# Two retention phases hand their PSUM banks over one by one, and a gated projection moves from the gate's chunks to a stretch of its own

## The reference, cut to what matters

```python
# first block, layer by layer (layer 0 for x and ctx, 512 rows; layer 1 for x, 256 rows)
hx = _rmsnorm(x, norm_w) * (1 + scale[:, None]) + shift[:, None]
a_h, a_b, a_c, a_z, q, k, v, r_z = _split_in(hx @ w_in)
q_h = _axial_rope(_heads(q), row_pos, col_pos)
k_h = _axial_rope(_heads(k), row_pos, col_pos) * k_scale
o = _bidir_retention(q_h, k_h, _heads(v), lg_f, lg_b, s_f, s_b)
y_ret = _ret_out(o, r_z, ret_norm_w)
x = x + gate[:, None] * (jnp.concatenate([y_conv, y_ret], axis=-1) @ w_out)
# end of the second block
x = x + rms_norm(f, ln_ffn_post[i])          # f = (silu(g) * u) @ w_down
gate = jax.nn.sigmoid(rms_norm(x, ln_pli[i]) @ w_pli_gate[i])
x = x + gate * (p[i] @ w_pli_proj[i])        # p is 256 x 256, w_pli_proj 256 x 2048
```

## Time and profile before

| what | us |
|---|---|
| median of 3 runs | 3027.54 (3026.38 to 3034.44) |
| the profiled execution, its own time | 3030.63 |
| its span, first to last instruction | 3028.8 |
| PE busy, share of the span | 2950.3, 97% |
| DVE busy | 1828.4, 60% |
| ACT busy | 1367.8, 45% |

### The profile page before, as it was taken

One profiled execution on the slowest core, in us unless ns is written; L12 is line 12 of the kernel. 1 busy time (PEld: TensorE's weight loads), 2 busy tenths in 40 slices (PEclk: granted clock), 3 DMA queues, 4 the chain that ended last, 5 costly groups with the idle time before them and its releaser, 6 DMA issues.

```text
span 3028.8 us, 41594 instructions
## 1 busy us (share of the span) xinstructions
PE 2950.3 (97%) x14729; PEld 2477.7 (82%) x14729; DVE 1828.4 (60%) x2315; ACT 1367.8 (45%) x1890; POOL 111.3 (4%) x114
## 2 busy tenths in 40 slices
PE   7999999999999999999999999999999999999999
PEld 4678887788887889988888899997788888878877
DVE  6878878788774345544445677665545445444454
ACT  6732222433343244434444577674544444434353
POOL 0000000000110000001110000000000000000000
PEclk9999999999999999999999999999999999999999
DMA  8855545444554225543334555555555555555545
GB/s 279 305 186 188 184 173 191 153 161 151 199 183 163 93 100 187 186 134 109 106 108 145 168 156 155 158 160 171 158 186 182 185 182 183 185 195 188 188 154 167
DMA packets 144277, 515.12 MB, mean 170 GB/s; under 512 B 16240, under 2 KB 16288, under 8 KB 142256
## 3 DMA queue, kind: packets, MB, share of 16 engines
q1 hardware_dynamic: 141264, 495.01, 49.2%
q0 software_dynamic: 2912, 18.74, 1.7%
HBM read 511.55 MB, written 2.13 MB: 170 GB/s over the span
## 4 chain that ended last, share of the span: by engine, by line
PE 57%; ACT 2%; DVE 2%; issue 2%; DMA 0%; ACTq 0%; DVEq 0%; SPq 0%
PE main L1582 47%; PE main L1575 6%; PE aux L1535 1%; ACT w_hi L580 1%; PE aux L1717 0%; PE aux L1708 0%; DVE w_lo L983 0%; PE aux L1555 0%; DVE h_lo L1105 0%; DMA raw<-in_w_sb 0%; ACT L804 0%; PE aux L1768 0%; ACT h_hi L690 0%; PE main L1655 0%; DVE u L1267 0%
## 5 line engine op out<-in xcount | busy, mean ns | idle before, releaser
L983 DVE TENSOR_TENSOR w_lo<-raw,w_hi 128x1024 fp32r<-128x1024 f32 x836 | 1039.1, 1246 | 876.2 <-ACT w_hi L580 865.7
L580 ACT ACTIVATE w_hi<-raw 128x1024 fp32r<-128x1024 f32 x836 | 880.1, 1058 | 1297.0 <-PE main L1582 973.8
L1582 PE MATMUL main<-w_hi,h_hi 128*128 128x512 f32 (+1 forms) x1472 | 561.9, 382 | 6.4 <-DVE h_lo L1232 3.1
L1582 PE MATMUL main<-w_lo,h_hi 128*128 128x512 f32 (+1 forms) x1472 | 552.4, 375 | 0.0
L1582 PE MATMUL main<-w_hi,h_lo 128*128 128x512 f32 (+1 forms) x1472 | 552.4, 375 | 0.0
L1582 PE MATMUL main<-w_hi,act_hi 128*128 128x512 f32 (+1 forms) x1408 | 536.4, 381 | 10.6 <-ACT u L720 6.5
L1582 PE MATMUL main<-w_hi,act_lo 128*128 128x512 f32 (+1 forms) x1408 | 528.2, 375 | 0.0
L1582 PE MATMUL main<-w_lo,act_hi 128*128 128x512 f32 (+1 forms) x1408 | 527.7, 375 | 0.0
L1575 PE MATMUL main<-act_hi,w_hi 128*128 128x256 f32 (+1 forms) x960 | 321.7, 335 | 3.7 <-DVE act_lo L1087 2.8
L1575 PE MATMUL main<-act_hi,w_lo 128*128 128x256 f32 (+1 forms) x960 | 320.5, 334 | 0.0
L1575 PE MATMUL main<-act_lo,w_hi 128*128 128x256 f32 (+1 forms) x960 | 320.4, 334 | 0.0
(11 more groups left out here) (269 smaller groups left out, 2491.2 us busy)
## 6 DMA issues: line engine op xcount, KB each, us to landing
raw<-in_w_ffn_up SPq DMA_DIRECT2D x176, 512.0 KB, 3.3
gates<-in_w_side SPq DMA_DIRECT2D x128, 512.0 KB, 3.4
raw<-in_w_in_ret SPq DMA_DIRECT2D x128, 512.0 KB, 4.0
raw<-in_w_in_conv SPq DMA_DIRECT2D x120, 512.0 KB, 4.1
raw<-in_w_out SPq DMA_DIRECT2D x96, 512.0 KB, 3.3
raw<-in_w_ffn_down SPq DMA_DIRECT2D x88, 512.0 KB, 4.2
raw<-in_w_mod SPq DMA_DIRECT2D x64, 512.0 KB, 4.7
raw<-in_w_sb SPq DMA_DIRECT2D x64, 384.0 KB, 3.1
```

Source lines behind the costliest of these rows:

```text
L580: A(w_hi[:, slot, :], raw[:, slot, :], ACT.Copy).then_inc(hi_split, 1)
L983: V.tensor_tensor(out=w_lo[:, slot, :], in0=raw[:, slot, :], in1=w_hi[:, slot, :].bitcast(F32), op=ALU.subtract).then_inc(lo_split, 1)
L1582: ins = mm(bank[:, c0:c1], x, w_part[:, slot, j * n + c0:j * n + c1], start=(k == 0 and j == 0 and i == 0), stop=(k == (7 if name == "gate ...
```

## The change

**Bank by bank.** In the last piece of every chunk of `in0_ret` and `in1_ret`, PE now signals `bank_done` after each of the banks 0, 1 and 2, as it did in `out0` only. ACT waits for the signal of bank 0 and of bank 2, DVE for that of bank 1; DVE's copy of bank 3 still waits for the whole chunk. The counts of `out0` are offset (`banks`).

**The projection.** The four pieces of `w_pli_proj` leave the gate's chunks and become a phase `proj` of 4 pieces between `ffn_down` and `gate`, whose chunks now have 8 pieces. PE runs two of them straight after `ffn_down`, one between the transposes of groups 0 and 1, and one behind those; the identity matmuls there are gone. ACT copies each product from `main` to a new SBUF tile `pp` (`proj_out`), and DVE multiplies by `pp` at the end. The fetch and the split of p move into the last chunk of `ffn_down`. Four splits of weight pieces on ACT and DVE now stand between the steps of the norm, where one stood behind the first two groups.

```diff
@@ -34,7 +34,8 @@
     ("in1_ret", 8, 8, 1024), ("out1", 4, 8, 1024), ("sb", 8, 8, 768), ("dil", 8, 8, 768),
-    ("out2", 4, 8, 1024), ("ffn_up", 22, 8, 1024), ("ffn_down", 4, 22, 1024), ("gate", 4, 9, 1024),
+    ("out2", 4, 8, 1024), ("ffn_up", 22, 8, 1024), ("ffn_down", 4, 22, 1024),
+    ("proj", 1, 4, 1024), ("gate", 4, 8, 1024),
 ]
@@ -267,6 +268,7 @@
         p_lo = sb(pli, "p_lo", [P, 2 * 256], F32R)
+        pp = sb(pli, "pp", [P, 2, D])
         pli.close()
@@ -321,13 +323,15 @@
             done_a[name], done_d[name] = na, nd
-            evacuated = {"mod0": 0, "in0_conv": 8}.get(name, c)
+            evacuated = {"mod0": 0, "in0_conv": 8, "proj": 0}.get(name, c)
             nd += evacuated
...
         paired = {n: n not in ("in0_conv", "in0_ret", "in1_ret", "out0") for n, *_ in PHASES}
+        banks = {"in0_ret": 0, "out0": 24, "in1_ret": 36}
@@ -557,7 +561,7 @@
             pool.dma_start(frow[:], a["rows"][2, :].partition_broadcast(P)).then_inc(s["fr_in"], 16)
-            pool.wait_ge(s["eaten"], chunk_end("ffn_down", 3))
+            pool.wait_ge(s["eaten"], chunk_end("ffn_down", 2) + 13)
             pool.dma_start(ptok[:], a["pT"]).then_inc(s["pt_in"], 16)
@@ -678,10 +682,10 @@
-            def prepare(n, A_cols, k):
+            def prepare(n, A_cols, k, groups=None):
                 j = prep_index(n) - 3
-                for kg in norm_groups(k):
+                for kg in norm_groups(k) if groups is None else groups:
                     m = 4 * prep_index(n) + kg
@@ -713,9 +717,9 @@
                 if k == 0:
-                    act.wait_ge(eaten, chunk_end(f"in{L}_ret", e))
                     act.wait_ge(s["rt_y"], 8 * L + e + 1)
                     for t in range(0, 4, 2):
+                        act.wait_ge(s["bank_done"], banks[f"in{L}_ret"] + 3 * e + t + 1)
                         lo, n = (128, 256) if t >= T else (0, 512)
@@ -955,18 +959,36 @@
             phase("ffn_up", lambda k: prepare(5, ln("ffnpre"), k), ffn_up)
-            phase("ffn_down", lambda k: ffn_up(21, 1, k), lambda e, par, k: plain_out("ffn_down", e, par, k))
+            def down_step(e, par, k):
+                plain_out("ffn_down", e, par, k)
+                if isinstance(e, int) and e == 2 and k == 17:
+                    act.wait_ge(s["pt_in"], 16)
+                    A(p_hi[:], ptok[:], ACT.Copy).then_inc(s["px_h"], 1)
+            def proj_out(k):
+                act.wait_ge(eaten, BASE["proj"] + k + 1)
+                for t in range(2):
+                    ins = A(pp[:, t, k * 512:(k + 1) * 512], main[2 * (k % 2) + t][:, :], ACT.Copy)
+                ins.then_inc(s["pj_done"], 1)
+            phase("ffn_down", lambda k: ffn_up(21, 1, k), down_step)
             sqrt_table()
...
             norm_root(6, 2)
-
-            def gate_start(k):
-                prepare(7, ln("pli"), k)
-                if k == 5:
-                    act.wait_ge(s["pt_in"], 16)
-                    A(p_hi[:], ptok[:], ACT.Copy).then_inc(s["px_h"], 1)
-
-            phase("gate", gate_start, gate, last=True)
+            first = BASE["proj"] + LEAD
+            split(first, first % SLOTS)
+            proj_out(0)
+            prepare(7, ln("pli"), 0, (0,))
+            split(first + 1, (first + 1) % SLOTS)
+            proj_out(1)
+            prepare(7, ln("pli"), 0, (1,))
+            split(first + 2, (first + 2) % SLOTS)
+            proj_out(2)
+            split(first + 3, (first + 3) % SLOTS)
+            proj_out(3)
+            phase("gate", lambda k: prepare(7, ln("pli"), k, () if k == 0 else None), gate, last=True)
             gate(3, 1, 0)
@@ -1119,7 +1141,19 @@
-                if k == 0:
+                if k == 0 and n == 7:
+                    first = BASE["proj"] + LEAD
+                    x_group(0)
+                    split(first, first % SLOTS)
+                    x_group(1)
+                    low(0)
+                    split(first + 1, (first + 1) % SLOTS)
+                    x_group(2)
+                    low(1)
+                    split(first + 2, (first + 2) % SLOTS)
+                    x_group(3)
+                    split(first + 3, (first + 3) % SLOTS)
+                elif k == 0:
                     x_group(0)
@@ -1171,8 +1205,11 @@
                 if k == 0:
-                    dve.wait_ge(eaten, chunk_end(f"in{L}_ret", e))
                     for t in (1, 3):
+                        if t == 1:
+                            dve.wait_ge(s["bank_done"], banks[f"in{L}_ret"] + 3 * e + 2)
+                        else:
+                            dve.wait_ge(eaten, chunk_end(f"in{L}_ret", e))
                         lo, w = (128, 256) if t >= T else (0, 512)
@@ -1248,7 +1285,7 @@
                         if L == 0:
-                            dve.wait_ge(s["bank_done"] if t < 3 else eaten, 3 * e + t + 1 if t < 3 else chunk_end("out0", e))
+                            dve.wait_ge(s["bank_done"] if t < 3 else eaten, banks["out0"] + 3 * e + t + 1 if t < 3 else chunk_end("out0", e))
                         ins = V.tensor_tensor(out=u[:, t, :], in0=main[(2 * par if L else 0) + t][:, :], in1=gt, op=ALU.mult)
@@ -1346,8 +1383,9 @@
                     dve.wait_ge(free_a, done_a["gate"] + e + 1)
+                    dve.wait_ge(s["pj_done"], e + 1)
                     for t in range(2):
-                        ch.link(V.tensor_tensor(out=sig[:, t, :], in0=sig[:, t, :], in1=aux[2 * par + t][:, :], op=ALU.mult))
+                        ch.link(V.tensor_tensor(out=sig[:, t, :], in0=sig[:, t, :], in1=pp[:, t, 512 * e:512 * (e + 1)], op=ALU.mult))
                     for t in range(2):
@@ -1512,19 +1550,16 @@
                 plain_out("ffn_down", frow, e, par, k)
+                if isinstance(e, int) and e == 2 and k == 18:
+                    dve.wait_ge(s["px_h"], 1)
+                    V.tensor_tensor(out=p_lo[:], in0=ptok[:], in1=p_hi[:].bitcast(F32), op=ALU.subtract).then_inc(s["p_ready"], 1)
...
-            def gate_start(k):
-                prepare(7, ln("pli"), residual, k)
-                if k == 5:
-                    dve.wait_ge(s["px_h"], 1)
-                    V.tensor_tensor(out=p_lo[:], in0=ptok[:], in1=p_hi[:].bitcast(F32), op=ALU.subtract).then_inc(s["p_ready"], 1)
-
-            phase("gate", gate_start, gate, last=True)
+            phase("gate", lambda k: prepare(7, ln("pli"), residual, k), gate, last=True)
             gate(3, 1, 0)
@@ -1546,18 +1581,10 @@
                 pe.wait_ge(lo_split, BASE[name] + c * per + k + 1)
-                if name == "gate" and k == 8:
-
-                    for t in range(2):
-                        for j in range(2):
-                            cs = slice(j * 256 + t * P, j * 256 + (t + 1) * P)
-                            for i, (x, w_part) in enumerate(((p_hi, w_hi), (p_hi, w_lo), (p_lo, w_hi))):
-                                ins = mm(aux[2 * (c % 2) + t][:, :], x[:, cs], w_part[:, slot, j * n:(j + 1) * n],
-                                         start=(j == 0 and i == 0), stop=(j == 1 and i == 2))
-                    ins.then_inc(eaten, 1)
-                    return
+                if name == "gate" and k == 0 and c < 2:
+                    pe.wait_ge(s["pj_done"], 3 + c)
                 for t, (bank, c0, c1, stat) in enumerate(parts):
-                    if name == "out0" and k == per - 1 and t > 0:
+                    if name in banks and k == per - 1 and t > 0:
                         ins.then_inc(s["bank_done"], 1)
@@ -1580,7 +1607,7 @@
                             ins = mm(bank[:, c0:c1], x, w_part[:, slot, j * n + c0:j * n + c1],
-                                     start=(k == 0 and j == 0 and i == 0), stop=(k == (7 if name == "gate" else per - 1) and j == 1 and i == 2))
+                                     start=(k == 0 and j == 0 and i == 0), stop=(k == per - 1 and j == 1 and i == 2))
                 ins.then_inc(eaten, 1)
@@ -1914,13 +1941,37 @@
             phase("ffn_down", lambda k: ffn_up(21, 1, k), lambda e, par, k: None, two(f_hi, f_lo), ready=down_ready)
-            gate_norm = norm_head(7, 2, None, "gate", (18, 6))
+            def proj(k):
+                if k < 2:
+                    pe.wait_ge(free_a, done_a["ffn_down"] + 3 + k)
+                    pe.wait_ge(free_d, done_d["ffn_down"] + 3 + k)
+                else:
+                    pe.wait_ge(s["pj_done"], k - 1)
+                pe.wait_ge(lo_split, BASE["proj"] + k + 1)
+                slot = (BASE["proj"] + k) % SLOTS
+                for t in range(2):
+                    for j in range(2):
+                        cs = slice(j * 256 + t * P, j * 256 + (t + 1) * P)
+                        for i, (x, w_part) in enumerate(((p_hi, w_hi), (p_hi, w_lo), (p_lo, w_hi))):
+                            ins = mm(main[2 * (k % 2) + t][:, :], x[:, cs], w_part[:, slot, j * 512:(j + 1) * 512],
+                                     start=(j == 0 and i == 0), stop=(j == 1 and i == 2))
+                ins.then_inc(eaten, 1)
```

(21 more changed lines are left out.)

## The result

The changed kernel takes **3015.26 us** (median of 6 runs, 3014.21 to 3017.88) beside 3028.69 us (6 runs, 3026.38 to 3034.44) of the kernel before: a ratio of 0.995, 95% interval 0.9939 to 0.996. In a second, later comparison it took 3015.68 beside 3033.06 (0.9937, 0.9924 to 0.995). It is faster, by 13 us in the first medians and 17 in the second; the prediction's sum was 16.05, its time 3011.5.

A forecast was written before the change was run, and what follows sets the result against it. The prediction took PE's stream, busy for 97% of the span, as the bound. Retention 9.8 plus projection 6.25 made 16.05 us, taken from a median of 3027.54 to give 3011.5 us, range 3006.5 to 3018.5.

The forecast's parts named there:

- Seven chunk ends of `in1_ret`: Behind chunks 0 to 6, PE's stalls on ACT's bank 0 copy go, 1.02 us each: 7.1 us saved.
- `in0_ret` 1.5 and the entry into `out0` 0.6: Stalls after chunks 5 and 6 of `in0_ret` save 1.5 us; PE's shorter wait on DVE into `out0` saves 0.60.
- The entry into `out1`: PE waits there only for DVE's second copy after the chunk's end, saving 0.61 us.
- The projection part: Gate loses 11.2 us of projection matmuls, the gap ahead of it grows 4.95 us: net 6.25 us saved.
- serial sum on ACT: Between `ffn_down` and the gate, ACT's steps in a row set the gate's start at 2924.0 instead of 2919.04.
- fetch and split of p: Moved into `ffn_down`'s last chunk, hidden by ACT's idle time and lead; without that cover it would cost 1.3 us.
- Rival (b): Projection part brings little: slower ACT steps or PE waiting for a split delay the gate; 3017.8 us, chance 0.12.
- The clock in the gap: Between `ffn_down` and the gate, PE's clock stays at 1.00 (2.4 GHz) without the identity matmuls.
- Rival (e): Slower than before: the clock falls to 1.2 GHz without identity matmuls, costing 11.2 us in the gap alone; chance 0.03.
- The signs: Expected in the profile: projection at 2899 or so, 15 us between `ffn_down` and gate, `pp` waited for last, gate matmuls 91.4 us.
- The sum: Whole kernel: retention 9.8 plus projection 6.25 gives 16.05 us saved.
- case (a): Both parts, retention and projection, work as worked out: 3008 to 3015 us, chance 0.68.

The follow-up runs named there:

- e4_dve_early: Changed kernel, but ACT waits for the whole chunk before both its copies in the retention phases, DVE copies bank 1 early: 3025.14 us, ratio 0.9978.
- e5_copy_first: Changed kernel, with ACT's third pair of projection copies ahead of a weight split instead of behind it: 3015.01 us, ratio 0.9938.
- e1_ret_only: Kernel before, with only the bank-by-bank signals of the retention phases, projection left in the gate: 3024.03 us, ratio 0.997.
- e2_proj_only: Changed kernel, with the retention phases waiting as before, so only the projection is moved: 3024.51 us, ratio 0.9977.
- e8_both: Changed kernel, with ACT's third copy pair ahead of a split and identity matmuls in three stalls: 3011.04 us, ratio 0.9923.

## Why the prediction was right

**Seven chunk ends of `in1_ret`**, 7 x 1.02 = 7.1: measured 7.15, `in1_ret` 38.14 us a chunk (38.15 said). That a stall shown as 0.77 costs 1.02, with the slow first matmul, held. The embedding is the next thing that could be late: DVE is done with it at 1379.15 and PE's transposes start at 1380.29, a slack of 1.14 us (1.15 said; rows of the timelines, as in the earlier trace rows):

```profile
1378.46 0.69 DVE L1226 TENSOR_TENSOR qk<-qk,sT 128x512 f32<-128x512 f32 x1
...
1380.29 0.60 PE L1570 MATMUL aux<-mats,qk 128*128 128x128 f32 x4
```

**`in0_ret` 1.5 and the entry into `out0` 0.6**: 2.1 said, 2.2 measured. **The entry into `out1`** 0.61: 0.60 measured (1.16 to 0.56). The first figure holds only because DVE's copy is early too: it also brings `kT` in time, and without it 0.55 us more would be lost. I had not seen that.

**The projection part**, 11.2 - 4.95 = 6.25: measured 11.2 - 4.35 = 6.85. The order of events was as written out, up to ACT as the engine waited for, at its copy `pp`. The term mis-sized is the serial sum on ACT, 14.9 us from the last `ffn_down` slot to the gate's start, measured 14.3. Up to ACT's first `h_hi` the forecast held within 0.1 us (7.1 said, 7.0 measured); behind it, 7.8 said were 7.3. I gave 0.2 us for the steps between its instructions. The timeline shows the reverse; each begins some 0.12 us before the one ahead is shown to end:

```profile
2910.25 1.57 ACT L694 ACTIVATE h_hi<-aux,cols 128x256 fp32r<-128x256 f32 x4 [1.73 <-PE aux L1570]
2911.69 1.07 ACT L584 ACTIVATE w_hi<-raw 128x1024 fp32r<-128x1024 f32 x1
2912.64 1.10 ACT L973 ACTIVATE pp<-main 128x512 f32<-128x512 f32 x2
2913.91 1.57 ACT L694 ACTIVATE h_hi<-aux,cols 128x256 fp32r<-128x256 f32 x4 [0.17 <-PE aux L1570]
```

So PE never waited ahead of its fourth projection piece, where I had 0.45 us; ACT even waited 0.17 us for PE's transposes, and the chain runs through PE up to there. The fetch and split of p cost PE nothing, as said: it waits for nothing from 2660 to 2903. Rival (b), that each step on ACT takes longer, went the other way.

**The clock in the gap**: kept at 1.00 in every run, as said. Rival (e) did not come. Where the clock does matter is at places that the change left alone and the prediction did not look at.

**The signs.** The gate's matmuls take 91.4 us, and 14.5 us lie between `ffn_down`'s last matmul and the gate's first (15 said), with `pp` the last wait. Only the projection stands at 2903.26 and not at some 2899, because the lead ahead of it was 5.8 us and not 9.8.

**The sum.** 16.05 said, 16.8 found in the changed stretches of the one pair of traces, 17.4 and 13.4 in the medians of the two comparisons. The time said, 3011.5, is 3.8 below the first median. The measured median is inside the range, but 0.3 above the 3008 to 3015 of case (a), although the mechanism is that case's. Two things make the difference. The sum was taken from the median of the three runs shown, 3027.54, which lies low: later medians of the same kernel are 3028.69, 3032.29 and 3033.06. And the sum took the rest of the program as fixed, although its time varies by a few microseconds from one execution to the next, at places that can be named in the trace. The medians' savings lie 2.6 below and 1.3 above the sum, so how near any one median comes to the forecast is in part luck; the agreement that counts is that of the terms.

## What to carry to other kernels

When a bank is filled before its neighbours, signal it then, and look which engine the next piece waits for first: here ACT's half gave 7 us and DVE's nothing by itself. A product that needs nothing from the steps around it belongs in the gap where PE multiplies for show; its price is what the serial engine of that gap gains in work, so write that engine's order out and put what PE waits for first in it. Before a change of 0.5% is judged by its medians, subtract PE's times at the same marks in both traces, part by part.

## What the runs showed of the hardware that I had not expected

**The clock falls behind stalls of 1.9 to 2.7 us, in some executions, and each fall costs 1.4 to 1.6 us.** Of the eight profiled executions without identity matmuls at these places, six have the slow matmuls behind the stall of 2.7 us ahead of `in1_conv` (the stretch to `in1_ret` then takes 1.4 to 1.5 us more), five behind the 2.0 us of `out2` (1.55) and five behind the 1.9 us of `ffn_down` (1.55 to 1.57). The changed kernel has the last and the one before does not, but `e4_dve_early` and `e5_copy_first`, which have the changed end, don't either, and `e1_ret_only`, which has the old one, does. In the two executions with identity matmuls there are none of the three. A fourth place is left as it was in all ten: behind a stall of 2.4 us at 540 the next stretch takes 20.7 to 20.8 us in eight executions, and 19.36 and 19.35 in `e2_proj_only` and `e8_both`, where the granted clock from 535 to 560 is 1.00 instead of 0.93. The Trainium skill, "TensorE: Matmul & The Clock Gate", section on HAM oscillation, has the mechanism, that stretches without matmuls send the clock back to half and each costs again. The traces agree with that, at some 1.5 us a time; but the waits in the section's case are longer than these stalls, and here a stall of 1.9 us was enough in five of eight executions. Why the same stall brings it in one execution and not in the next stays open.

**One transfer takes 6.9 to 9.1 us**, 9.1 and 7.4 in two executions of the same program, and PE has no slack for it. Behind the stall the clock can fall as well: in `e1_ret_only` and in `e5_copy_first` the window from 1730 to 1740 is at 0.83, in the changed kernel at 1.00. From PE's matmul that starts at 1734.03 in before to the mark at 1791.49 those two take 60.5 and 60.2 us, the changed kernel 59.0, before 57.5. The row is that of `e1_ret_only`:

```profile
1730.00:1740.00 10.00, 9.38 (x33) 6.35 (x34) 5.92 (x8) 3.53 (x4) 0.00 (x0) 0.83 0.38 107
```
